# Hybrid attention and gated-MLP layer on one core: the stores of probabilities and normed outputs move from SyncE's queue to ScalarE's

## What is computed

```
h = rms_norm(x) * norm1_g
proj = h @ w_in                      # q, k, v of 8 forgetting heads and of 8 differential heads
forgetting head:   p = softmax(q k^T * scale + c_q - c_k, causal);           o = p v
differential head: a = softmax(q1 k1^T) - lam * softmax(q2 k2^T), by chunks; o = rms_norm(a v) * gain
x = x + concat(o) @ w_out
u = rms_norm(x) @ w_up               # 2 x 5504 columns, then a causal depthwise convolution of width 3
x = x + (silu(gate) * value) @ w_down
```

## Time and profile before

| | |
|---|---|
| median of 3 runs | 1043.76 us (1042.52 to 1043.76) |
| the profiled execution, its own time | 1045.0 us |
| its span, from the first instruction to the last | 1043.2 us |
| PE busy | 1037.5 us (99% of the span) |
| ACT busy | 784.3 us (75%) |
| DVE busy | 750.9 us (72%) |
| mean share of the 16 DMA engines, SP's queue | 65.5% |
| granted clock of TensorE | 1.00 throughout |

### The profile page before, as it was taken

How to read it: one execution, slowest core, us unless ns; L and a number is a source line. 1 busy time by engine, 2 the same in 40 slices (tenths; PEclk the granted TensorE clock), 3 DMA queues, 4 the chain that set the end, 5 groups by cost and what they waited for, 6 DMA issues and landing times.

```text
span 1043.2 us, 16400 instructions
## 1 busy us (share of the span) xinstructions
PE 1037.5 (99%) x5302; PEld 939.5 (90%) x5302; DVE 750.9 (72%) x1258; ACT 784.3 (75%) x1379; POOL 21.0 (2%) x27
## 2 busy tenths in 40 slices
PE   9999999999999999999999999999999999999998
PEld 8999999999988888888888888888889988888887
DVE  6888878868776665577786776876867678766664
ACT  6776776888858885879779788798797778755553
POOL 0101010000000000000000000000000000000000
PEclk9999999999999999999999999999999999999999
DMA  9667777777766666666666665565656666666664
GB/s 353 236 187 219 218 238 224 224 241 234 243 234 200 202 203 202 201 203 205 195 220 191 198 221 186 197 221 186 217 183 199 226 204 205 203 201 208 206 202 143
DMA packets 81436, 221.04 MB, mean 212 GB/s; under 512 B 20312, under 2 KB 24544, under 8 KB 81248
## 3 DMA queue, kind: packets, MB, share of 16 engines
q1 hardware_dynamic: 81232, 220.07, 65.5%
q10 hardware_dynamic: 144, 0.20, 0.1%
HBM read 214.32 MB, written 5.91 MB: 211 GB/s over the span
## 4 chain that ended last, share of the span: by engine, by line
PE 87%; DVE 5%; ACT 4%; DMA 2%; issue 1%; SPq 0%; DVEq 0%; ACTq 0%
PE ps L653 14%; PE ps L655 14%; PE ps L654 14%; PE ps L683 7%; PE ps L684 7%; PE ps L682 7%; PE ps L444 4%; PE ps L446 4%; PE ps L445 4%; PE ps L632 3%; PE ps L633 3%; PE ps L634 3%; DVE w_lo L1178 2%; DMA raw<-in_win 1%; ACT qkT L780 1%
## 5 line engine op out<-in xcount | busy, mean ns | idle before, releaser
L1178 DVE TENSOR_TENSOR w_lo<-raw,w_hi 128x1024 fp32r<-128x1024 f32 (+1 forms) x406 | 462.6, 1144 | 240.8 <-ACT w_hi L730 238.2
L730 ACT ACTIVATE w_hi<-raw 128x1024 fp32r<-128x1024 f32 (+1 forms) x406 | 397.6, 987 | 170.1 <-PE ps L684 74.7
L653 PE MATMUL ps<-w_hi,xs 128*128 128x512 f32 (+1 forms) x704 | 263.4, 374 | 0.0
L654 PE MATMUL ps<-w_lo,xs 128*128 128x512 f32 (+1 forms) x704 | 263.4, 374 | 0.0
L655 PE MATMUL ps<-w_hi,xs 128*128 128x512 f32 (+1 forms) x704 | 263.4, 374 | 0.0
L444 PE MATMUL ps<-w_hi,xs 128*128 128x384 f32 (+1 forms) x496 | 165.0, 333 | 0.8 <-DVE w_lo L1178 0.7
L445 PE MATMUL ps<-w_lo,xs 128*128 128x384 f32 (+1 forms) x496 | 161.8, 326 | 0.0
L446 PE MATMUL ps<-w_hi,xs 128*128 128x384 f32 (+1 forms) x496 | 161.8, 326 | 0.0
L654 PEld LDWEIGHTS ps<-w_lo,xs 128*128 128x128 f32 x704 | 133.1, 189 | 17.2
L653 PEld LDWEIGHTS ps<-w_hi,xs 128*128 128x128 f32 x704 | 133.1, 189 | 17.2
L655 PEld LDWEIGHTS ps<-w_hi,xs 128*128 128x128 f32 x704 | 133.1, 189 | 17.2
(11 more groups left out here) (171 smaller groups left out, 944.0 us busy)
## 6 DMA issues: line engine op xcount, KB each, us to landing
raw<-in_wrest SPq DMA_DIRECT2D x278, 512.0 KB, 3.6
raw<-in_win SPq DMA_DIRECT2D x117, 384.0 KB, 3.8
raw<-in_wrest SPq DMA_DIRECT2D x16, 384.0 KB, 3.0
p_scratch<-pdT SPq DMA_DIRECT2D x14, 192.0 KB, 3.3
p_read<-p_scratch SPq DMA_DIRECT2D x56, 48.0 KB, 2.6
xtok<-in_xtok SPq DMA_DIRECT2D x4, 512.0 KB, 12.9
xv<-in_xtok SPq DMA_DIRECT2D x4, 512.0 KB, 5.4
raw_ahead<-in_w SPq DMA_DIRECT2D x5, 392.0 KB, 8.5
```

The costliest lines, as they stand in the source:

```text
L653: pe.matmul(o, xh, wh, start=(k == 0), stop=False, skip_group_check=True)
L654: pe.matmul(o, xh, wl, start=False, stop=False, skip_group_check=True)
L730: act.activation(slot(w_hi, s, w), slot(raw, s, w), ACT.Copy).then_inc(hi_ready, 1)
L1178: dve.tensor_tensor(slot(w_lo, s, w), slot(raw, s, w), f32(slot(w_hi, s, w)), ALU.subtract).then_inc(split_done, 1)
```

## The change

`store_p` and `store_o` go from SP's program to ACT's. The instructions are the same DMAs with the same two waits each: one for DVE's turn, one for the landing of the loads of the trip before. On ACT `store_o(f - 2)` stands at the end of step 2, behind `copy_p`, and `store_p(f)` at the end of step 5 (of step 7 in frames 10 to 15). The reads and the loads of the pieces stay in SP's queue in their old order.

```diff
@@ block.sync
-            def store_p(f):
-                sp.wait_ge(p_turned, bounced(f))
-                if f > P0:
-                    sp.wait_ge(p_landed, 64 * bounced(f - 1))
-                sp.dma_start(p_d, pdT[:]).then_inc(p_stored, 16)
-            def store_o(f):
-                sp.wait_ge(o_turned, f)
-                if f > 1:
-                    sp.wait_ge(o_landed, 64 * (f - 1))
-                sp.dma_start(o_d, onT[:]).then_inc(o_stored, 16)
...
-                    if f == 2 and b == 7:
-                        store_p(2)
...
-                        if b == 2:
-                            store_o(1)
...
-                        if b == 5:
-                            store_p(3)
...
-                    if 4 <= f <= H + 2 and b == 1:
-                        store_o(f - 2)
...
-                    if 4 <= f <= H + 1 and b == 4:
-                        store_p(f)
...
-                    if H + 1 < f < P_STOP and b == 6:
-                        store_p(f)
@@ block.scalar
+            def store_p(f):
+                act.wait_ge(p_turned, bounced(f))
+                if not (isinstance(f, int) and f == P0):
+                    act.wait_ge(p_landed, 64 * f - 64 * P0)
+                act.dma_start(p_d, pdT[:]).then_inc(p_stored, 16)
+            def store_o(f):
+                act.wait_ge(o_turned, f)
+                if f > 1:
+                    act.wait_ge(o_landed, 64 * (f - 1))
+                act.dma_start(o_d, onT[:]).then_inc(o_stored, 16)
...
                     if forget:
                         forget_steps(b)
+                    if isinstance(f, int) and f <= H + 2 and b == 2:
+                        store_o(f - 2)
+                    if b == (7 if at is BLOCK_AT else 5):
+                        store_p(f)
...
                 if b == 7:
                     head_norm(3, "diff")
+                    store_p(2)
...
+                if b == 2:
+                    store_o(1)
                 if b == 3:
                     copy_qkT(3, "diff")
                     copy_p(2, unscaled=True)
...
                 if b == 5:
                     out_sums(2)
+                    store_p(3)
```

## The result

| | before | changed |
|---|---|---|
| median of 6 runs | 1043.09 us (1042.52 to 1043.76) | 1050.58 us (1050.37 to 1051.57) |
| ratio, 95% interval | | 1.007 (1.006 to 1.008) |
| span of the profiled execution | 1043.2 us | 1048.6 us |

A forecast was written before the change was run, and what follows sets the result against it. PE was taken to bound the kernel, busy 268.53 of 270.00 us. Terms 6.20 (store_o) - 0.7 (absorbed wait) + 0.2 (store_p) = 5.7 us, added to a 1043.8 us median: 1049.5 us, range 1046.0 to 1053.5.

The forecast's parts named there:

- PE sets the end, and nothing is to be gained.: From 40 to 310 us PE is busy 268.53 of 270.00 us; a better schedule could win only 1.47 us.
- `store_o` in frames 3 to 9, 1.93 us from the turn to the scores.: Step 2: ACT waits for DVE's turn of onT, so PE's scores start 1.93 us after it; 6.20 us lost together.
- The losses add up.: Frames 3 to 9: each loss on PE delays the next frame equally and nothing later catches up; 6.20 us in sum.
- The 0.79 us that PE loses ahead of it come off that wait, all 0.7 us of it.: Behind frame 7's scores: PE's 0.7 us wait for w_lo absorbs that frame's loss, giving back 0.7 us.
- I count 0.2 us there, and nothing in the others.: store_p in step 5 makes L761 0.21 us late; PE meets it once, at the w_lo wait's place, for 0.2 us.
- The price of an issue, 0.41 us.: One DMA issue in ACT's queue, from ACT's only one in the trace: 0.41 us, none of it hidden.
- The stores in a queue of their own free SP and land sooner.: Rival, faster: reads and late loads no longer stand behind stores on SP and come sooner; at most 1042.6 us, chance 0.02.

The follow-up runs named there:

- e1_o_only: The changed kernel with the 14 p stores given back to SP, only the 8 o stores on ACT: 1049.29 us against 1043.22 for the kernel before.
- e10_p_in_idle_time: The changed kernel with the p store behind ACT's split of step 6 instead of ahead of it: 1048.82 us, 5.9 us slower than the kernel before.
- e5_issue_only: The kernel before, plus a 64 KB store on ACT at the end of step 2 of frames 3 to 10 that waits for nothing: 1043.13 us against 1043.66.
- e4_o_behind_copies: The changed kernel with the o store at the end of step 3, behind the copies of qkT: 1044.07 us against 1043.22 for the kernel before.
- e6_two_issues: The changed kernel plus a spare 64 KB store right behind each o store on ACT: 1054.27 us against 1043.66 for the kernel before.
- e7_o_ahead_of_split: The changed kernel with the o store ahead of ACT's split of step 2 and copy_p in frames 3 to 9: 1058.37 us, 14.7 us slower than the kernel before.

## Why the prediction was right, and what was mis-sized

- *PE sets the end, and nothing is to be gained.* Right: no arrangement of the stores came out faster, PE's idle time in the stretch being 1.2 to 1.5 us.
- *`store_o` in frames 3 to 9, 1.93 us from the turn to the scores.* Right: 1.98 to 1.99 us was measured in frames 3 and 5 to 8, 1.84 us in frame 9 and 2.27 us in frame 4. The sum of seven waits was 6.8 us, with 6.20 forecast; the largest miss of a single one is frame 4, 0.66 us for 0.07. That it is a wait and what stands behind it is shown from several sides: the wait alone costs 3.4 us, the issue alone nothing that shows, another issue or two more activations behind the wait add their own time, and the store at a place with its data ready costs nothing.
- *"The losses add up."* Right; they persist to the end, which came 7.5 us later.
- *"The 0.79 us that PE loses ahead of it come off that wait, all 0.7 us of it."* This term failed. The wait was one of that execution, and not of the kernel, as its second profile shows. But the late load behind it had also put 1.39 us instead of 0.92 us (157.40 + 1.93 - 158.41) into the sum for frame 8; 0.89 and 0.90 us were measured there in e1_o_only and e10_p_in_idle_time. The two errors go against each other, and together they are 0.2 us. That the profiled execution was 1.2 us above the median of the runs is no sign of either: it comes from the start of the program.
- *"I count 0.2 us there, and nothing in the others."* The step on the p stores was right in its mechanism (L737 does start later, by 0.27 us, with 0.21 forecast) and wrong in where that arrives. I looked for it at DVE's last split of the frame, which has cover. It arrives through DVE's list at the turn of `onT` in the next frame, for which ACT now waits: the two moves share a path. e10_p_in_idle_time puts this term at 1.1 us by the medians, instead of 0.2. It is the largest error of the sum, and most of the way from 5.7 us to the 7.1 and 7.5 us measured. What is left are small errors in both directions (frame 4 too low, frame 9 too high).
- *The price of an issue, 0.41 us.* Right behind a wait, 0.43 us; but it was taken to be that of any issue, and it is zero where ACT's queue runs ahead of its engine. The rule that I cited (the Trainium skill, Perfetto Trace Analysis, DMA Instruction — HWDGE: wait, generation and release take place in the issuing sequencer one after the other) holds for the sequencer; what I made of it, that nothing of the issue is hidden, holds only while ACT's engine has nothing left to do, as behind the wait.
- *The stores in a queue of their own free SP and land sooner.* SP's waits for them did go, but no wait of PE with them, as forecast for this rival.

## What to carry to other kernels

A DMA that waits for another engine belongs in the list of an engine that has nothing else behind it, or behind the point at which its data are surely ready. What it costs elsewhere is read from the trace before: the end of what it waits for, plus the time from there through everything that stands behind it to the next instruction of the bounding engine, less where that starts now. Terms that rest on a late load, those that give time back above all, should show in more than one execution, and two small delays on one engine should be followed until it is known that they do not meet.

## What the runs showed that was not expected

An issue from ACT's queue costs 0.43 to 0.49 us behind a wait and nothing beside running activations (e5_issue_only, e4_o_behind_copies).

In the profile of e6_two_issues, the clock granted to TensorE fell for 3.4 us. PE had been busy for 2.37 of the 4 us before it, with its longest idle times of all these kernels but e7_o_ahead_of_split:

```profile
164.00:168.00 4.00, 2.37 (x19) 1.85 (x18) 2.23 (x4) 2.21 (x4) 0.00 (x0) 1.00 0.85 226
168.00:172.00 4.00, 4.00 (x16) 4.00 (x16) 2.85 (x14) 2.60 (x13) 0.00 (x0) 0.58 0.67 181
```

A mean of 0.58 is the 1.2 GHz level for most of the stretch. Its matmuls start 0.32 us apart there; those of the same form start 0.16 us apart where the granted clock is 1.00, the 2.4 GHz level:

```profile
168.03 0.53 PE L422 MATMUL ps<-w_lo,xs 128*128 128x384 f32 x1
168.35 0.53 PE L423 MATMUL ps<-w_hi,xs 128*128 128x384 f32 x1
```

That costs that execution up to 1.7 us, part of which comes off its last wait (0.9 us in frame 9). The one run of this kernel at a mean clock of 1.00 took 1054.15 us, the three at 0.998 took 1054.22 to 1055.23 us. The profile of e7_o_ahead_of_split, with longer waits, has the clock at 1.00 throughout, while the three other runs of that kernel had 0.995 to 0.998. So the same kernel comes with the fall and without it, and how much idle time brings it on is not settled by these runs.
